# Norms of h by token halves at six boundaries, and row spreads of the second layer by transfers through device memory

## The reference

```python
for l in range(2):                        # DEPTH
    hn = rms_norm(h, g_ffn1[l]) * (1.0 + sc1) + sh1
    h = h + 0.5 * (1.0 + gt1) * swiglu(hn, w_ffn1_in[l], w_ffn1_out[l])     # D_FF = 2816
    hn = rms_norm(h, g_mix[l]) * (1.0 + sc2) + sh2
    proj = hn @ w_mix_in[l]
    y = [sliding_window_sink_attention, rwkv7_time_mix, short_conv_mix](parts of proj)
    h = h + (1.0 + gt2) * (concatenate(y) @ w_mix_out[l])
    hn = rms_norm(h, g_ffn2[l]) * (1.0 + sc3) + sh3
    h = h + 0.5 * (1.0 + gt3) * swiglu(hn, w_ffn2_in[l], w_ffn2_out[l])
...
hn = rmsnorm(h) ; proj = hn @ w_in                                          # second_block
wts = softmax(lses over 3 groups)                                           # 8 heads x 512 tokens each
o_a = sum_g wts[g] * dilated_attention(g)                                   # dilations 1, 4, 16
o_b = gated_delta_rule(l2norm(q), l2norm(k), v, g, beta)                    # 8 heads of 64, chunks of 64
merged = sigmoid(gate_a) * ((o_a * silu(z_a)) @ w_up_a) + sigmoid(gate_b) * ((rmsnorm(o_b) * silu(z_b)) @ w_up_b)
out = rmsnorm(h + merged @ w_out)
```

## Time and profile before

| | us |
|---|---|
| runs | 2841.89, 2843.71, 2850.3 (median 2843.71) |
| profiled execution | 2850.33 |
| its span | 2847.6 |
| its mean granted clock | 0.969 |

### The profile page before, as it was taken

How to read it: one execution, slowest core, us unless ns; L and a number is a source line. 1 busy time by engine, 2 the same in 40 slices (tenths; PEclk the granted TensorE clock), 3 DMA queues, 4 the chain that set the end, 5 groups by cost and what they waited for, 6 DMA issues and landing times.

```text
span 2847.6 us, 42312 instructions
## 1 busy us (share of the span) xinstructions
PE 2739.9 (96%) x17748; PEld 2244.1 (79%) x17748; DVE 1491.7 (52%) x1860; ACT 963.2 (34%) x1472; POOL 187.4 (7%) x263
## 2 busy tenths in 40 slices
PE   6999999989999999999999999999999999989998
PEld 5888877787888878888877787888877777668787
DVE  6565575755555434333347744333365556665534
...
GB/s 290 189 217 206 189 168 79 63 3 97 206 204 225 104 102 89 81 111 91 101 76 75 18 46 81 82 110 103 82 113 113 101 110 67 52 13 4 58 102 74
DMA packets 51129, 305.97 MB, mean 107 GB/s; under 512 B 7200, under 2 KB 7328, under 8 KB 22688
## 3 DMA queue, kind: packets, MB, share of 16 engines
q1 hardware_dynamic: 41760, 236.65, 24.4%
q0 software_dynamic: 9216, 67.11, 6.5%
...
## 4 chain that ended last, share of the span: by engine, by line
PE 90%; DVE 6%; ACT 1%; DMA 1%; issue 1%; POOL 0%; SPq 0%; DVEq 0%; ACTq 0%
PE ps L932 18%; PE ps L934 18%; PE ps L933 17%; PE ps L1220 6%; PE ps L1221 6%; PE ps L1222 6%; PE ps L1566 2%; PE ps L1567 2%; PE ps L1568 2%; PE ps L2111 1%; PE ps L2095 1%; PE ps L2108 1%; DMA ada_first<-in_ada 1%; DVE w_lo L908 1%; DVE tmp L887 1%; PE ps L1302 1%
## 5 line engine op out<-in xcount | busy, mean ns | idle before, releaser
L932 PE MATMUL ps<-hn_hi,w_hi 128*128 128x512 f32 x1440 | 564.4, 392 | 19.1 <-DVE hn_lo L881 18.7
L933 PE MATMUL ps<-hn_lo,w_hi 128*128 128x512 f32 x1440 | 563.2, 391 | 0.0
L934 PE MATMUL ps<-hn_hi,w_lo 128*128 128x512 f32 x1440 | 562.8, 391 | 0.0
L908 DVE TENSOR_TENSOR w_lo<-w_raw,w_hi 128x2048 fp32r<-128x2048 f32 (+2 forms) x227 | 467.8, 2061 | 163.5 <-ACT w_hi L901 163.5
L901 ACT ACTIVATE w_hi<-w_raw 128x2048 fp32r<-128x2048 f32 (+2 forms) x227 | 390.7, 1721 | 106.6 <-PE ps L1222 103.9
L932 PEld LDWEIGHTS ps<-hn_hi,w_hi 128*128 128x128 f32 x1440 | 272.2, 189 | 78.2 <-issue 21.0
L1220 PE MATMUL ps<-hn_hi,w_hi 128*128 128x512 f32 x776 | 319.7, 412 | 8.7 <-DVE hn_lo L881 4.9
L933 PEld LDWEIGHTS ps<-hn_lo,w_hi 128*128 128x128 f32 x1440 | 272.4, 189 | 56.6
L934 PEld LDWEIGHTS ps<-hn_hi,w_lo 128*128 128x128 f32 x1440 | 272.1, 189 | 56.9
L1221 PE MATMUL ps<-hn_lo,w_hi 128*128 128x512 f32 x776 | 309.7, 399 | 0.0
L1222 PE MATMUL ps<-hn_hi,w_lo 128*128 128x512 f32 x776 | 308.7, 398 | 0.0
...
## 6 DMA issues: line engine op xcount, KB each, us to landing
w_raw<-in_up SPq DMA_DIRECT2D x88, 1024.0 KB, 4.9
ada_w<-in_ada POOLq DMA_DIRECT2D x64, 1024.0 KB, 5.2
...
w_raw<-in_mix_in SPq DMA_DIRECT2D x20, 1024.0 KB, 4.9
w_raw<-in_dsa_in SPq DMA_DIRECT2D x18, 1024.0 KB, 5.3
...
ada_first<-in_ada SPq DMA_DIRECT2D x8, 1024.0 KB, 12.4
w_raw<-in_mix_out SPq DMA_DIRECT2D x8, 1024.0 KB, 4.8
```

The source lines that it names most:

```text
L908: dve.tensor_tensor(w_lo[:, slot, 0:size], w_raw[:, slot, 0:size], w_hi[:, slot, 0:size].bitcast(F32), ALU.subtract).then_inc(w_lo_ready, 1)
L932: pe.matmul(bank, wh, x_hi[:, k], start=(k == 0), stop=False)
L933: pe.matmul(bank, wh, x_lo[:, k], start=False, stop=False)
L934: return pe.matmul(bank, wl, x_hi[:, k], start=False, stop=(k == K - 1))
```

## The change

It has three parts.

(1) At n = 1 to 6 the last piece of the sub-block ("tail": the last down piece, or the last of w_mix_out), the norm, and the first piece of the next sub-block are computed in two halves of 256 tokens. The tail's products run for tokens 0 to 255, then for 256 to 511, twice as many and half as wide. ACT evacuates and squares, and DVE updates h, by halves. The sums and the transposes of half 0 stand among the tail's products of half 1, those of half 1 among the first piece's of half 0. The norm's operations are 256 columns wide, 32 on DVE in the place of 16:

```diff
+        def tail_ffn_pe(pe, n):
+
+            p = tail_of(n)[1]
+            slot = p % 2
+            pe.wait_ge(w_lo_ready, p + 1)
+            pe.wait_ge(act_evac, p - 1)
+            pe.wait_ge(dve_evac, p - 1)
+            for hf in range(2):
+                for k in range(HALF):
+                    wh, wl = w_hi[:, slot, k * P:(k + 1) * P], w_lo[:, slot, k * P:(k + 1) * P]
+                    last = split_products(pe, main[slot][hf][:, cols(hf)], wh, wl, act_hi[:, k, cols(hf)], act_lo[:, k, cols(hf)],
+                                          k == 0, k == HALF - 1)
+                    if hf == 0 and k == 5:
+                        pe.wait_ge(sq_added, SQ_ADDS * n)
+                        early_sums_pe(pe, n, rstd[:], True)
+                    if hf and k == 2:
+                        tail_sums_pe(pe, n, 0)
+                    if hf and k == 5:
+                        tail_spread_pe(pe, n, 0)
+                if hf == 0:
+                    last.then_inc(tail_done, 1)
+                    pe.wait_ge(sq_ready, squares_before(n) + KD - 1)
+                    early_sums_pe(pe, n, norm_squares(n)[:, (KD - 2) % 2], False)
+            last.then_inc(piece_done, 1)
...
+        def first_halves_pe(pe, n, p, narrow):
+
+            slot = p % 2
+            pe.wait_ge(w_lo_ready, p + 1)
+            pe.wait_ge(act_evac, p - 1)
+            pe.wait_ge(dve_evac, p - 1)
+            for hf in range(2):
+                for k in range(KD):
+                    pe.wait_ge(hn_ready, hn_before(n, hf) + k + 1)
+                    for t in range(2):
+                        col = (2 * k + t) * P
+                        last = split_products(pe, ps[:, t, cols(hf)] if narrow else main[slot][t][:, cols(hf)],
+                                              w_hi[:, slot, col:col + P], w_lo[:, slot, col:col + P], hn_hi[:, k, cols(hf)],
+                                              hn_lo[:, k, cols(hf)], k == 0, k == KD - 1)
+                        if hf and k == KD - 1 and (t or narrow):
+                            last.then_inc(piece_done if t else first_done, 1)
+                    if hf == 0 and k == 2:
+                        tail_sums_pe(pe, n, 1)
+                    if hf == 0 and k == 5:
+                        tail_spread_pe(pe, n, 1)
```

(`tail_mix_pe` is the same with two output tiles, 24 products for each tile and half.) ACT's and DVE's order through a norm:

```diff
+        def norm_halves_act(act, n, shift):
+
+            def high(hf, j):
+                act.wait_ge(hn_tmp, hn_before(n, hf) + j + 1)
+                if shift is None:
+                    act.activation(hn_hi[:, j, cols(hf)], tmp[:, j % 2, cols(hf)], ACT.Copy).then_inc(hn_hi_ready, 1)
+                else:
+                    act.activation(hn_hi[:, j, cols(hf)], tmp[:, j % 2, cols(hf)], ACT.Identity,
+                                   bias=shift[:, j:j + 1]).then_inc(hn_hi_ready, 1)
+            tail_root_act(act, n, 0)
+            high(0, 0)
+            tail_evac_act(act, n, 1)
+            high(0, 1)
+            tail_square_act(act, n, 1)
+            high(0, 2)
+            high(0, 3)
+            tail_root_act(act, n, 1)
+            for j in range(4, KD):
+                high(0, j)
+            for j in range(KD):
+                high(1, j)
...
+        def norm_halves_dve(dve, n, shift):
+
+            def scaled(hf, j):
+                if j >= 2:
+                    dve.wait_ge(hn_ready, hn_before(n, hf) + j - 1)
+                dve.scalar_tensor_tensor(tmp[:, j % 2, cols(hf)], h[:, j, cols(hf)], norm_gain[:, j:j + 1], small[2 * hf][:, cols(hf)],
+                                         ALU.mult, ALU.mult).then_inc(hn_tmp, 1)
+
+            def low(hf, j):
+                dve.wait_ge(hn_hi_ready, hn_before(n, hf) + j + 1)
+                hi = hn_hi[:, j, cols(hf)].bitcast(F32)
+                if shift is None:
+                    dve.tensor_tensor(hn_lo[:, j, cols(hf)], tmp[:, j % 2, cols(hf)], hi, ALU.subtract).then_inc(hn_ready, 1)
+                else:
+                    dve.scalar_tensor_tensor(hn_lo[:, j, cols(hf)], tmp[:, j % 2, cols(hf)], shift[:, j:j + 1], hi,
+                                             ALU.add, ALU.subtract).then_inc(hn_ready, 1)
+            tail_rstd_dve(dve, n, 0)
+            for hf in range(2):
+                dve.wait_ge(norm_spread, norm_count(n, hf))
+                scaled(hf, 0)
+                for j in range(1, KD):
+                    scaled(hf, j)
+                    low(hf, j - 1)
+                    if hf == 0 and j == 1:
+                        tail_update_dve(dve, n, 1)
+                    if hf == 0 and j == 4:
+                        tail_rstd_dve(dve, n, 1)
+                low(hf, KD - 1)
```

In layer 0 the last ada piece before the mix moves from the down piece to behind the norm, ahead of DVE's splits of the mix:

```diff
             norm_dve(dve, own, 3 * l + 1, gains[:, l, 1], mods(l, 4), mods(l, 3))
+            if l == 0:
+                dve_ada(dve, ADA_BEFORE_MIX - 1)
```

(2) The selector products for the group weights, key norm, beta and decays are gone. POOL stores the rows in device memory and reads them back spread over 64 partitions, 1 MB for each of six sets of rows; DVE multiplies from SBUF. The product of the attention output by silu(z) goes from DVE to POOL (`gated_pool`), and so does the queries' product by the decays (`gd_read_pool`):

```diff
+        def mix_spread_pool(pool, at, group):
+
+            rows = mix_rows[:, group].rearrange("(a h j) t -> a h j t", a=2, h=2)
+            for hp in range(2):
+                for a in range(2):
+                    pool.dma_start(row_spread[at][half(hp), 2 * a:2 * a + 2],
+                                   rows[a, hp:hp + 1].broadcast_to([HD, 2, T])).then_inc(row_spread_in[at], 16)
+
+        def head_spread_pool(pool, dest, which, landed):
+
+            rows = gd_head_rows[which].rearrange("(j h) t -> h j t", h=2)
+            for hp in range(2):
+                pool.dma_start(dest[half(hp)], rows[hp:hp + 1].broadcast_to([HD, PAIRS, T])).then_inc(landed, 16)
+
+        def spread_rows_pool(pool):
+
+            pool.wait_ge(dsa_weights, 1)
+            pool.dma_start(mix_rows[:], ds_max[0:8]).then_inc(rows_out, 16)
+            pool.wait_ge(rows_out, 16)
+            mix_spread_pool(pool, 0, 0)
+            pool.wait_ge(gd_sums, 4)
+            mix_spread_pool(pool, 1, 1)
+            pool.wait_ge(gd_roots, 1)
+            pool.dma_start(gd_head_rows[1], gd_rows[0:8, 0]).then_inc(rows_out, 16)
+            pool.dma_start(gd_head_rows[2], restart[32:40]).then_inc(rows_out, 16)
+            pool.wait_ge(dsa_mixed, 1)
+            mix_spread_pool(pool, 0, 2)
+            pool.wait_ge(gd_k_rooted, 1)
+            pool.dma_start(gd_head_rows[0], gd_rows[32:40, 1]).then_inc(rows_out, 16)
+            pool.wait_ge(rows_out, 64)
+            pool.wait_ge(dsa_mixed, 2)
+            head_spread_pool(pool, row_spread[1], 0, row_spread_in[1])
+            head_spread_pool(pool, gd_kbg, 2, gd_decays_in[1])
+            gd_e_pool(pool, 0)
+            pool.wait_ge(dsa_mixed, 3)
+            head_spread_pool(pool, row_spread[0], 1, row_spread_in[0])
+            head_spread_pool(pool, gd_qd, 2, gd_decays_in[0])
+
+        def gated_pool(pool):
+
+            pool.wait_ge(dsa_z_ready, 1)
+            pool.tensor_tensor(ds_q[0][:], ds_q[0][:], ds_z[:], ALU.mult).then_inc(ya_f_ready, 1)
+
+        def gd_read_pool(pool, j):
+
+            pool.wait_ge(gd_decays_in[0], 32)
+            pool.tensor_tensor(gd_qd[:, j], gd_kq[:, 1, j], gd_qd[:, j], ALU.mult).then_inc(gd_read_ready, 1)
 
```

```diff
+        def mix_group_dve(dve, own, group):
+
+            at = 1 if group == 1 else 0
+            w, y, o, d = row_spread[at], ds_q[0], ds_q[group], DILATION[group]
+            dve.wait_ge(row_spread_in[at], 128 if group == 2 else 64)
             if group == 0:
-                dve.tensor_tensor(y, y, w, ALU.mult).then_inc(dsa_mixed, 1)
+                dve.tensor_tensor(y[:], y[:], w[:], ALU.mult).then_inc(dsa_mixed, 1)
                 return
-            d = DILATION[group]
-            t = ds_turned[h]
-            natural = lambda ap: ap.rearrange("p j (i r) -> p j i r", r=d)
-            for j in range(2):
-                last = dve.tensor_tensor(t[:, j].rearrange("p (i r) -> p i r", r=d), o[:, j].rearrange("p (r i) -> p i r", r=d),
-                                         w[:, j].rearrange("p (i r) -> p i r", r=d), ALU.mult)
-            last.then_inc(dsa_mixed, 1)
-            dve.wait_ge(dsa_mixed, part + 1)
-            own(dve.tensor_tensor(y, y, t[:], ALU.add))
+            for j in range(PAIRS):
+                by_token = w[:, j].rearrange("p (i r) -> p i r", r=d)
+                last = dve.tensor_tensor(by_token, o[:, j].rearrange("p (r i) -> p i r", r=d), by_token, ALU.mult)
+            own(last)
+            dve.wait_ge(dsa_mixed, group)
+            dve.tensor_tensor(y[:], y[:], w[:], ALU.add).then_inc(dsa_mixed, 1)
```

```diff
-            mix_dve_part(dve, own, 0)
-            mix_dve_part(dve, own, 1)
             dve.wait_ge(gd_roots, 1)
             dve.reciprocal(g_rows[:, 1], g_rows[:, 1]).then_inc(gd_k_rooted, 1)
+            mix_group_dve(dve, own, 0)
             second_evac_dve(dve, pz + 1, ds_z[:, 3:4])
             split_dve(dve, *whole(pg + 1))
-            mix_dve_part(dve, own, 2)
-            mix_dve_part(dve, own, 3)
+            mix_group_dve(dve, own, 1)
+            mix_group_dve(dve, own, 2)
             second_evac_dve(dve, pg, gz(1).rearrange("p (a t) -> p a t", a=1))
-            mix_dve_part(dve, own, 4)
-            mix_dve_part(dve, own, 5)
```

(42 more changed lines are left out.)

532 lines of the change are left out of this document (303 added, 229 removed).

## The result

The changed kernel takes 2804.49 us (median of four runs, 2803.25 to 2812.18); the kernel before takes 2842.8. The ratio is 0.987 (95% interval 0.9851 to 0.9889): 38 us faster. The profiled execution has a span of 2802.8 us; that of before had 2847.6, in an execution 7.5 us above the median.

A forecast was written before the change was run, and what follows sets the result against it. PE (96% busy, 90% of the last chain) and its holes bound the kernel, with DVE's chain at boundaries. Terms -18-6-6.3-5-6-2.5+10 = -34 from the 2843.7 median gave 2810 us; range 2768 to 2838.

The forecast's parts named there:

- part 2: GDN row spreads go through memory instead of PE's selector products: -18 us to the first mask, -6 in the first set.
- Halves: Six boundaries: DVE starts 3.9 us earlier but needs 14.6 us instead of 11.6; windows 186.6 us, before 181.6.
- Rival (a): Six boundaries: with halves DVE keeps up and PE streams, 39 us less than before, kernel 2761; chance 0.12.
- The clock behind a boundary: Slow products after PE's idle hole ahead of the second piece: 5 us added for six boundaries (0 to 12).
- Spreads, to the first mask: Second layer, weights' end to first GDN mask: six 1 MB spreads in one POOL queue, 18 us less (7 to 26).
- POOL's product by z is hidden: Before the first GDN mask: POOL's 5 us product runs beside the wait for beta's spread; without that cover 2 us.
- First GDN set: First mask to first right-hand side: decay products and two waits go, 6 us less (3 to 9).
- Attention: Both mixes: scores ahead of turns remove the six 1.1 us waits for att_s, 6.4 us less (4 to 6.5).
- RWKV: Both layers' RWKV mixes: start 5 us less (2 to 7), end 6 us less (3 to 14).
- dense products may lift it, worth up to 5 a layer; I take 1.2: RWKV end: dense products beside four chunks may raise the clock, 0.74 there; 1.2 us a layer taken.
- Its start: RWKV start: holes before the levels shrink, masks start at 568 instead of 573.1; 2.5 us a layer.
- GDN end: End of the GDN delta: 6 products into holes, no wait for the last outputs, 2.5 us less (1 to 4).

The follow-up runs named there:

- whole boundaries: Changed kernel with all six boundaries back in whole tokens, spreads and small parts kept: 2792.1 us, ratio 0.981.
- filled halves: Changed kernel plus 12 unread products of 512 columns behind the first piece of each of the six boundaries: 2799.2 us, ratio 0.9833.
- the kernel with beta early: Changed kernel with beta spread next to the key norm, and decays spread once for both decayed products: 2808.4 us, ratio 0.9869.

## Why the prediction was right

2810 us and -34 were forecast, 2804.5 and -38 measured. Part 1 cost time and part 2 gave most, by the steps described. But several terms were off, and the sum is good in part by luck: the misses in the ledger are +6.0 us (clock behind the boundaries, attention) against -17 (RWKV, both GDN stretches, the start), -11 in all, and the profiled execution of before stood 7.5 us above its median.

- **Halves.** The step held as written: DVE started 3.9 us earlier, then had twice as many operations at 0.455 us (forecast 0.457), products at 0.120 (0.120), idle 2.6 to 4.2 us against 2.9 and 4.4. The six windows lie within 0.6 us of their forecasts, the mix kind above (33.6 for 33.1) and the others below (31.1 to 28.9 for 31.4 to 29.2), so that the sum, 186.6, is exact by chance. That part 1 costs time was the forecast (+10), and whole boundaries show it (17 by the ratios, 13 between the spans). Rival (a) is out.
- **The clock behind a boundary** was mis-sized: 5 forecast, 8.6 measured. At five boundaries it was 1.6 to 2.1 us, and one, the second, had none. The filled halves show the cause, the hole; why the second had none is open.
- **Spreads, to the first mask.** Forecast 41.4 us after the weights' end for beta's landing, measured 41.5; first mask 18.0 us earlier, as forecast. This is luck in part: three terms were off and cancelled. The first spread landed 12.7 us after the weights' end instead of 10.4. The third group took 7.5 us instead of 4.2, because POOL worked beside it, which I had at nothing. And beta's transfer took 7.3 us from its issue instead of 12.5; it was issued 9.5 us behind the keys' and 8.2 behind the decays' (these take 9.4 to land), so there was next to nothing ahead of it any more. That POOL's product by z is hidden held only because DVE waited for a transfer anyway. Without that cover I had 2 us; the kernel with beta early shows 4.2.
- **First GDN set.** -7.8 in a range of -3 to -9; 26.9 us from mask to right-hand side instead of 34.7.
- **Attention.** The waits went as forecast (6.4 to 1.3; undoing the order costs 7). Ahead of them the guests' sums and the products behind them lost 1.8 and 1.7 us, at a lower clock than before, which was not in the sum.
- **RWKV** was the largest miss: 11 forecast, 18.8 measured. At its end the step "dense products may lift it, worth up to 5 a layer; I take 1.2" had the mechanism, and took a part of it: 6 forecast for both layers, 10 measured. With the products the clock stays at 1.00 in the chunks and in the group norm behind, and taking them away brings back 10 us in the traces and 11 by the ratios. Its start gave 8.6 for 5; no run separates what did that.
- **GDN end**: 2.5 forecast, 8.5 measured. Here the cause is not shown. 4.6 us of it lie in the merge stretch, which runs at clock 1.00 in seven of the twelve traces that have the edit and at less in five, so this execution was one of the lucky ones.
